# Turning the expert activations in squares of 32 on VectorE and ScalarE in place of four TensorE transposes

## The reference

```python
top_vals, top_idx = lax.top_k(logits, TOP_K)            # TOP_K = 4 of 32 experts
top_w = jax.nn.softmax(top_vals, axis=-1)
combine = jnp.sum(one_hot(top_idx, 32) * top_w[..., None], axis=1)
for e in range(N_EXPERTS):
    gt = jnp.minimum(t @ exp_w_gate[e] + exp_b_gate[e], 7.0)
    up = jnp.clip(t @ exp_w_up[e] + exp_b_up[e], -7.0, 7.0)
    act = gt * jax.nn.sigmoid(1.702 * gt) * (up + 1.0)
    out = out + combine[:, e:e + 1] * (act @ exp_w_down[e] + exp_b_down[e])
```

## Time and profile before

| | us |
|---|---|
| median of 3 runs | 1191.56 (1186.92 to 1192.03) |
| the profiled execution, its own time | 1192.14 |
| its span, first to last instruction | 1189.4 |
| TensorE busy (matmuls) | 1144.3, 96% of the span |
| TensorE weight loads | 455.4, 38% |
| VectorE busy | 473.6, 40% |
| ScalarE busy | 202.5, 17% |
| DMA, mean over the span | 383 GB/s, 456.09 MB |
| granted TensorE clock, mean | 0.99 |

### The profile page before, as it was taken

One profiled execution on the slowest core, in us unless ns is written; L12 is line 12 of the kernel. 1 busy time (PEld: TensorE's weight loads), 2 busy tenths in 40 slices (PEclk: granted clock), 3 DMA queues, 4 the chain that ended last, 5 costly groups with the idle time before them and its releaser, 6 DMA issues.

```text
span 1189.4 us, 16024 instructions
## 1 busy us (share of the span) xinstructions
PE 1144.3 (96%) x5982; PEld 455.4 (38%) x5983; DVE 473.6 (40%) x1074; ACT 202.5 (17%) x371; POOL 46.6 (4%) x80
## 2 busy tenths in 40 slices
PE   8999999999999999999999999999999999999993
PEld 5675666633333333333333333333333333333321
DVE  3499315553333333333333333333333333333337
ACT  2001311222112111111111121121111111111112
POOL 4054000100000000000000000000000000000000
PEclk9999999989999999999999999999999999999997
DMA  9967558299999999999999999999999999999992
GB/s 347 372 252 281 223 202 319 94 400 408 428 428 428 428 428 429 429 428 428 429 429 429 379 408 429 428 430 427 429 428 428 429 427 429 428 429 429 427 430 88
DMA packets 53665, 456.09 MB, mean 383 GB/s; under 512 B 5321, under 2 KB 20229, under 8 KB 27019
## 3 DMA queue, kind: packets, MB, share of 16 engines
q1 hardware_dynamic: 51392, 452.87, 91.9%
q10 hardware_dynamic: 2251, 2.93, 0.9%
HBM read 454.38 MB, written 1.40 MB: 383 GB/s over the span
## 4 chain that ended last, share of the span: by engine, by line
PE 67%; DMA 23%; DVE 8%; SPq 1%; issue 1%; ACT 0%; ACTq 0%; DVEq 0%
PE bank L1643 43%; DMA ring<-in_exp_w_gate 14%; DMA arena<-in_exp_w_gate 6%; DVE h L896 5%; PE bank L1676 4%; PE bank L1594 4%; PE bank L1411 3%; DMA ring<-mod_rows 2%; PE bank L1514 2%; PE bank L1723 1%; DMA ring<-in_w_ada 1%; PE bank L1498 1%; PE bank L1602 1%; PE bank L1663 1%; PE bank L1360 1%; SPq L442 1%
## 5 line engine op out<-in xcount | busy, mean ns | idle before, releaser
L1643 PE MATMUL bank<-ring,arena 128*64 128x512 f32 x2368 | 531.2, 598 | 13.8 <-DMA ring<-in_exp_w_gate 12.2
L1643 PEld LDWEIGHTS bank<-ring,arena 128*64 128x64 f32 x2368 | 162.9, 137 | 355.3 <-issue 314.7
L1643 PE MATMUL bank<-arena 128*64 128x512 f32 x800 | 179.3, 596 | 3.3 <-DMA arena<-in_exp_w_gate 3.3
L1171 DVE TENSOR_SCALAR arena<-bank 128x512 f32<-128x512 f32 x33 | 22.8, 692 | 296.6 <-PE bank L1643 296.6
L754 ACT ACTIVATE arena<-arena 32x256 f32<-32x256 f32 x136 | 56.0, 412 | 432.0 <-DVE arena L1100 430.8
L1156 DVE TENSOR_TENSOR arena<-arena,bank 128x512 f32<-128x512 f32 x132 | 84.8, 684 | 110.8 <-PE bank L1676 79.4
L1643 PEld LDWEIGHTS bank<-arena 128*64 128x64 f32 x800 | 54.8, 137 | 118.0 <-issue 107.0
L1676 PE MATMUL bank<-arena 64*128 64x512 f32 x264 | 74.5, 641 | 0.0
L1594 PE MATMUL bank<-h,arena 128*64 128x512 f32 x272 | 64.4, 593 | 0.2 <-DVE arena L1023 0.2
L1411 PE MATMUL bank<-arena,ring 128*128 128x288 f32 x256 | 64.0, 408 | 0.0
L896 DVE SCALAR_TENSOR_TENSOR h<-h,arena 128x318 f32<-128x318 f32 x120 | 61.9, 595 | 0.0
(11 more groups left out here) (299 smaller groups left out, 774.3 us busy)
## 6 DMA issues: line engine op xcount, KB each, us to landing
ring<-in_exp_w_down SPq DMA_DIRECT2D x48, 2048.0 KB, 26.5
ring<-in_exp_w_gate SPq DMA_DIRECT2D x48, 2048.0 KB, 24.0
ring<-in_exp_w_up SPq DMA_DIRECT2D x48, 2048.0 KB, 25.7
arena<-in_exp_w_gate SPq DMA_DIRECT2D x16, 2048.0 KB, 22.9
arena<-in_exp_w_up SPq DMA_DIRECT2D x16, 2048.0 KB, 28.0
arena<-in_exp_w_down SPq DMA_DIRECT2D x16, 2048.0 KB, 26.6
ring<-in_w_ada SPq DMA_DIRECT2D x24, 1024.0 KB, 9.4
ring<-in_gate_w SPq DMA_DIRECT2D x8, 1024.0 KB, 7.0
```

What stands on the lines that cost most here:

```text
L1643: ins = mm(out[64 * hh:64 * hh + 64, :], lhs(k), w[:, D * (k % 2) + HALF * hh:D * (k % 2) + HALF * (hh + 1)], start=(done is y_mm and k == ...
```

## The change

`acts` is no longer turned by TensorE. VectorE turns it in squares of 32 into a new buffer `act_sq`, exactly as it does with the tokens, and the squares are moved into `actT` by four copies on VectorE (partitions 0 to 63) and four on ScalarE (64 to 127). ScalarE's four stand between its sigmoid and the moves of the next tokens. TensorE goes from `gather` directly to `gather_end`, and waits for both halves (`actT_dve`, `actT_act`) before the down product. So that the turned squares are in the right order of rows, the gate and up columns and their bias rows are split over the two halves as the tokens are: half 0 computes columns 0 to 255 and 512 to 767. The down product's columns are as before. Instruction counts in an item: TensorE 4 transposes fewer; VectorE one copy of 128 x 512 fewer, one turn of 128 x 512 and four copies of 32 x 256 more; ScalarE four copies of 32 x 256 more.

```diff
+        act_sq = view(12480, HALF)
...
-        def square_moves(hh, s, u):
-
-            src = xg[64 * hh + 32 * s:64 * hh + 32 * s + 32, :].rearrange("p (h u r j) -> p h u r j", h=2, u=2, r=4)[:, :, u, :, :]
-            dst = xgT[64 * hh + 32 * u:64 * hh + 32 * u + 32, :].rearrange("p (h r s j) -> p h r s j", h=2, r=4, s=2)[:, :, :, s, :]
+        def square_moves(hh, s, u, turned_sq, out):
+
+            src = turned_sq[64 * hh + 32 * s:64 * hh + 32 * s + 32, :].rearrange("p (h u r j) -> p h u r j", h=2, u=2, r=4)[:, :, u, :, :]
+            dst = out[64 * hh + 32 * u:64 * hh + 32 * u + 32, :].rearrange("p (h r s j) -> p h r s j", h=2, r=4, s=2)[:, :, :, s, :]
...
-            def move_squares():
+            def move_squares(turned_sq, out, done):
                 for s, u in ((0, 0), (1, 0), (0, 1), (1, 1)):
-                    ins = a.activation(*square_moves(1, s, u), ACT.Copy)
-                ins.then_inc(xgT_act, 1)
+                    ins = a.activation(*square_moves(1, s, u, turned_sq, out), ACT.Copy)
+                ins.then_inc(done, 1)
...
                 a.activation(gsig, gmin, ACT.Sigmoid, scale=ALPHA).then_inc(gsig_ready, 1)
+                act.wait_ge(act_turned, n + 1)
+                move_squares(act_sq, actT, actT_act)
                 act.wait_ge(xg_ev, n + 2)
-                move_squares()
+                move_squares(xg, xgT, xgT_act)
...
                                        op0=ALU.add, op1=ALU.mult).then_inc(act_ready, 1)
-                dve.wait_ge(actT_mm, n_e + 1)
-                v.tensor_copy(actT, bank[2][:, :]).then_inc(actT_ev, 1)
+                dve.wait_ge(act_ready, n_e + 1)
+                v.transpose(act_sq, blocks(acts)).then_inc(act_turned, 1)
+                dve.wait_ge(act_turned, n_e + 1)
+                for s, u in ((0, 0), (1, 0), (0, 1), (1, 1)):
+                    ins = v.tensor_copy(*square_moves(0, s, u, act_sq, actT))
+                ins.then_inc(actT_dve, 1)
...
-                    mm(bank[3][out, :], mine[B_GATE, :], bias_rows[B_GATE, cs], start=True, stop=False, skip_group_check=True)
-                    mm(bank[4][out, :], mine[B_UP, :], bias_rows[B_UP, cs], start=True, stop=False, skip_group_check=True)
+                    mm(bank[3][out, :], mine[B_GATE, :], half_rows(bias_rows[B_GATE, :], hh), start=True, stop=False, skip_group_check=True)
+                    mm(bank[4][out, :], mine[B_UP, :], half_rows(bias_rows[B_UP, :], hh), start=True, stop=False, skip_group_check=True)
...
+                    row = w[:, D * (k % 2):D * (k % 2 + 1)]
                     for hh in range(2):
-                        ins = mm(out[64 * hh:64 * hh + 64, :], lhs(k), w[:, D * (k % 2) + HALF * hh:D * (k % 2) + HALF * (hh + 1)],
+                        cut = row[:, HALF * hh:HALF * (hh + 1)] if done is y_mm else half_rows(row, hh)
+                        ins = mm(out[64 * hh:64 * hh + 64, :], lhs(k), cut,
...
                 gather(n + 1, piece_used)
-                pe.wait_ge(act_ready, n + 1)
-                pe.wait_ge(actT_ev, n + 1)
-                for q in range(4):
-                    ins = tr(bank[2][:, P * q:P * (q + 1)], row_order(acts, q), ident[:, :])
-                ins.then_inc(actT_mm, 1)
                 gather_end(n + 1)
 
-                pe.wait_ge(actT_ev, n + 2)
+                pe.wait_ge(actT_dve, n + 1)
+                pe.wait_ge(actT_act, n + 1)
                 pe.wait_ge(scat_add, n * 2 + 2)
-                product(bank[5], lambda k: half_of(actT, k), g, j, 8, y_mm)
+                product(bank[5], lambda k: actT[:, 64 * k:64 * k + 64], g, j, 8, y_mm)
```

More of the change, by code:

```diff
@@ L339, in build @@
         act_ready = sem("act_ready")
-        actT_mm = sem("actT_mm")
-        actT_ev = sem("actT_ev")
+        act_turned = sem("act_turned")
+        actT_dve = sem("actT_dve")
+        actT_act = sem("actT_act")
         y_mm = sem("y_mm")
@@ L369, in build @@
         wd_v = exp_w_down[0].rearrange(rows_of, h=2, r=4)
-        def row_order(ap, j):
-            return ap.rearrange("p (q j) -> p q j", j=4)[:, :, j]
         def half_rows(ap, hh):
@@ L1065, in _ @@
             v.tensor_scalar(mine[:, :], part_no[:, :], 0.0, None, ALU.is_equal).then_inc(mine_ready, 1)
-            for free in (gate_read, up_read, scat_add, actT_ev):
+            for free in (gate_read, up_read, scat_add):
                 dve.sem_inc(free, 1)
@@ L1102, in turn_tokens @@
                 for s, u in ((0, 0), (1, 0), (0, 1), (1, 1)):
-                    ins = v.tensor_copy(*square_moves(0, s, u))
+                    ins = v.tensor_copy(*square_moves(0, s, u, xg, xgT))
                 ins.then_inc(xgT_dve, 1)
@@ L1600, in gather_strips @@
                 for hh in range(2):
-                    out, cs = slice(64 * hh, 64 * hh + 64), slice(HALF * hh, HALF * (hh + 1))
-                    mm(bank[3][out, :], mine[B_GATE, :], bias_rows[B_GATE, cs], start=True, stop=False, skip_group_check=True)
-                    mm(bank[4][out, :], mine[B_UP, :], bias_rows[B_UP, cs], start=True, stop=False, skip_group_check=True)
+                    out = slice(64 * hh, 64 * hh + 64)
+                    mm(bank[3][out, :], mine[B_GATE, :], half_rows(bias_rows[B_GATE, :], hh), start=True, stop=False, skip_group_check=True)
+                    mm(bank[4][out, :], mine[B_UP, :], half_rows(bias_rows[B_UP, :], hh), start=True, stop=False, skip_group_check=True)
                     if lookup:
@@ L1652, in product @@
                 ins.then_inc(done, 1)
-            def half_of(buf, k):
-                return buf[:, P * (k % 4) + 64 * (k // 4):P * (k % 4) + 64 * (k // 4) + 64]
             def scatter_sample():
```

## The result

The changed kernel takes 1199.99 us (median of 6 runs, 1198.94 to 1203.95) against 1191.66 us before (6 runs, 1186.92 to 1192.29): slower by 0.87%, the ratio being 1.0087 with a 95% interval of 1.0066 to 1.0108. In a second session, beside the experiments, it took 1203.10 against 1191.29 (ratio 1.0100, interval 1.0083 to 1.0117). The forecast of 1195.9 had the direction; the time lies in its range of 1189.5 to 1203, past the 6 us at which the prediction's rival A begins, and twice as far from the start as forecast (8.3 us for 4.3).

What follows compares the result with a forecast made beforehand. TensorE (27.29 us an item) and the weight DMA (29.3 us an expert) run side by side, with DMA waits covering 6.9 and 12.0 us. At d = 0.70, 16d - 6.9 = 4.3 us on 1191.56 gives 1195.9, range 1189.5 to 1203.

Steps and rivals of the forecast that it cites:

- rival A: At the seam, the turn reading SBUF four elements apart makes d 0.78 or more, slower by over 0.5%; chance 0.20.
- The two covers of 6.9 and 12.0 us: TensorE's lateness from DMA waits at items 14 and 32, under which a longer item costs nothing: 6.9 and 12.0 us.
- d: Delay of the down product's start in each item, forecast at 0.70 us, bounds 0.60 to 0.95.
- the rule: Cost over the span: 16d - 6.9 for d of 0.53 to 0.75, three times d below, 32 us per further microsecond above.
- 33d: Rival in the experiments: TensorE's time simply counts in each of the 33 items; no chance given.
- The chain: From L1178 through VectorE's turn and ScalarE's copies to the down product: 4.13 us, against 3.43 before.
- Only the turn has no exact twin: VectorE's turn out of SBUF lacks a trace row of the same shape; taken as 0.72 us from the PSUM token turn.
- The way from ScalarE to TensorE: Time from the end of ScalarE's four copies to TensorE's start on the down product, taken as 0.24 us.
- The sum: Total delay over the span: 16d - 6.9 = 4.3 us at d = 0.70.
- B: Rival at the seam: the chain is hidden and TensorE keeps its 0.68 us, gaining 2.0 us, 1189.5; chance 0.06.
- C: Rival: the 1.38 us gap before each down product costs TensorE its clock, 2.9 us an item, 1292; chance 0.03.
- D: Rival in gate and up products: columns in two runs of 256 stream 4% slower, 0.56 us an item, 1213; chance 0.03.

Runs made afterwards that it cites:

- the plain turn: The changed kernel with VectorE's turn reading acts in plain order instead of four elements apart: 1194.12 us against 1191.64 for the kernel before, ratio 1.0018.
- the kernel without transposes: The kernel before with its four TensorE transposes left out, VectorE copying acts to actT unturned: 1189.01 us against 1191.64, ratio 0.9961.

## Why the prediction was right or wrong

**What bounds the kernel: right, and it carried everything else.** The two covers of 6.9 and 12.0 us, read off two rows, account for the loop of the changed kernel to 0.2 us (15 x 1.00 - 6.9 = 8.1 for 7.9). Four variants with an average d of 0.33, 0.44, 0.60 and 0.60 came out 0.9, 1.1, 2.8 and 2.5 us above the kernel before, where the rule gives 1.0, 1.3, 2.7 and 2.7. With d = -0.68 it was 2.6 us below, for 2.0 forecast. These medians are uncertain by 1.5 us and more either way, so they exclude 33d but don't fix the covers; the traces do: in the plain turn the issues that are 416.45 us apart before are 418.26 apart, 1.8 more, and 15 x 0.60 - 6.9 is 2.1.

**The chain: the mechanism right, one term mis-sized.** The step that failed is "Only the turn has no exact twin", with its 0.72 us and the bounds of 10% upward. It measures 1.12. I had read the difference to the twin as SBUF against PSUM, and that costs nothing; what matters is the step of four elements, which out of PSUM is free and out of SBUF is not. I had named the step under rival A and found no row with it; the bound should then not have been 10%. The way from ScalarE to TensorE was a little shorter than the 0.24 taken, 0.10 and 0.19 us in the two kinds of items. Together d became 1.00 for 0.70, outside the bounds of 0.60 to 0.95.

**The sum: sensitive as stated, and inside its range by luck.** By its own formula for both covers used up, d = 1.00 gives 32 - 18.9 = 13.1 us, or 1204.7, outside the range. One term was missed: once DMA no longer sets the end, VectorE doesn't wait for mod_rows either, a third cover of 1.20 us, so that 11.9 remain. The two profiled spans differ by 12.6, of which 1.2 arise before the loop: 11.4. The two sessions gave 8.3 and 11.8 us, the first with executions of the changed kernel 5 us apart (1198.94 to 1203.95). It is this spread that brought the first median into the range; the second, 1203.10, lies just outside. And the likeliest outcome, no change beyond 0.5% (0.71), is not what came: the interval of 0.66% to 1.08% is the case that had 0.26.

**The rivals.** A is what happened, through the mechanism it named, the step of four elements in SBUF, though with a turn of 1.12 us (d = 1.00) and not one twice as long (d = 1.42). B's price is confirmed by the kernel without transposes. C does not occur here but is real: 0.2 to 0.3 us more would have set it off. The dense work ahead of the gap, which the prediction held against it, kept the clock at gaps of up to 1.68 us and no longer did in 25 of 33 items at 1.88 to 1.99. Its price of 2.9 us an item was too high; 1.5 to 1.7 us is measured. The row it was taken from, item 0's product, has the clock low from 243 to 250 us; here it is low about half as long (back at 1.00 some 3 us after the product that starts at 702.35). D is excluded.

**What would show it.** Items of 27.99 us were named as the test, 28.29 came. The DMA waits before gate weights did vanish, altogether and not nearly. The last dip of the DMA rate came at 698 to 700 us (188 GB/s) and not near 692; 16 x 1.00 - 6.9 = 9.1 us and the 1.2 us before the loop, added to the 688 of the kernel before, put it there. L1649's mean stayed at 598 ns, the clock in the loop at 1.00 and the steady DMA rate at 429 GB/s.

## What to carry to other kernels

When an engine and the DMA stream are nearly equally fast, find the rows where the one was last late for the other: the waits at these points are a budget, all but free up to their size and charged for every item beyond, and they also cap what a saving can bring. A turn that must read with a step of four should read PSUM, not SBUF (copies with such a step were not compared), so place the reordering in the instruction that takes the data out of PSUM anyway. And before work is moved off TensorE onto a chain it must wait for, compare the gap that this makes with the gaps after which the clock was seen to fall, for a delay on one side of that point costs its own length, and on the other side it cost 2.6 times that (81 us for 31) and some 5 times (48 to 52 for 10).

## What the runs showed of the hardware

- VectorE's turn of 128 x 512 fp32 takes 0.71 us from contiguous SBUF, 0.72 from PSUM with a step of four elements, and 1.12 from SBUF with that step. Clipping out of PSUM takes 0.69 us with and without the step.
- A plain copy of 128 x 512 fp32 from SBUF to SBUF takes VectorE 0.43 us (the kernel without transposes), one out of PSUM 0.69.
- After dense work, gaps of TensorE of up to 1.68 us in each item left the granted clock at 1.00 in every item; after gaps of 1.88 to 1.99 us it fell to 0.50 in 25 of 33 items, in some only after the next product had begun, and after 2.51 to 2.64 us in all.
- The profile names VectorE as the releaser of TensorE's wait for two semaphores, although ScalarE's copies ended 0.5 us later and taking two of them away moved TensorE.
